# Split fp32r products and gathered experts against plain fp32 products and experts over all tokens

## The reference, cut to what matters

```python
for layer in range(2):                       # first model
    h = rms_norm(x, norm_w)
    proj = h @ w_in                          # 1024 x 12832
    y_a = mamba2_branch(...)                 # convolution, chunked scan, 16 heads
    y_b = sliding_window_branch(...)         # rope, 16 heads, window 128
    y_c = forgetting_attention_branch(...)   # 16 heads
    merged = sum(sigmoid(gate_i) * (y_i @ w_proj[i]))
    x = x + merged @ w_out
x = rms_norm(x, final_norm_w)
# second model: sparse top-64 attention, attention to a memory of 256, S5 state space,
# mixed as above, then the mixture of experts:
combine = ...                                # 256 x 32, two nonzero weights a token
for e in range(32):
    hid = silu(t @ w_gate[e]) * (t @ w_up[e])          # 1024 x 512 each
    out = out + combine[:, e:e + 1] * (hid @ w_down[e])  # 512 x 1024
```

## Time and profile before

| | |
|---|---|
| median of 3 runs | 2602.28 us (2600.16 to 2602.51) |
| profiled execution, own time | 2604.87 us |
| its span | 2603.1 us |
| mean granted clock of PE | 0.888 |
| busy: PE, DVE, ACT, POOL | 2142.0, 1513.6, 1197.3, 898.8 us |
| read from HBM | 406.23 MB |

### The profile page before, as it was taken

One profiled execution on the slowest core, in us unless ns is written; L12 is line 12 of the kernel. 1 busy time (PEld: TensorE's weight loads), 2 busy tenths in 40 slices (PEclk: granted clock), 3 DMA queues, 4 the chain that ended last, 5 costly groups with the idle time before them and its releaser, 6 DMA issues.

```text
span 2603.1 us, 26970 instructions
## 1 busy us (share of the span) xinstructions
PE 2142.0 (82%) x10022; PEld 1737.6 (67%) x10022; DVE 1513.6 (58%) x2250; ACT 1197.3 (46%) x1786; POOL 898.8 (35%) x417
## 2 busy tenths in 40 slices
PE   6796998999878699899765276447689999999997
PEld 5575776677657577667654255335578888888885
DVE  1666232432166623244784645893478888888885
ACT  4342443333333244333324234102457777777774
POOL 4562653346456265334435124643300000000000
PEclk8897998899789799899877687777889999999998
DMA  5342442233434244223333112132469999999994
GB/s 168 99 121 74 131 129 81 81 98 121 130 106 122 74 128 128 77 89 116 105 100 102 49 49 88 66 113 65 145 221 335 328 332 335 322 336 332 324 335 164
DMA packets 137450, 411.15 MB, mean 158 GB/s; under 512 B 20572, under 2 KB 21980, under 8 KB 110184
## 3 DMA queue, kind: packets, MB, share of 16 engines
q1 hardware_dynamic: 132280, 407.31, 47.6%
q0 software_dynamic: 5040, 2.12, 0.3%
HBM read 406.23 MB, written 19.40 MB: 164 GB/s over the span
## 4 chain that ended last, share of the span: by engine, by line
PE 70%; DVE 23%; ACT 4%; issue 2%; DMA 1%; POOL 0%; SPq 0%; DVEq 0%; ACTq 0%; POOLq 0%
PE bank L518 18%; PE bank L519 17%; PE bank L520 17%; DVE r L945 9%; PE bank L830 3%; PE bank L497 2%; DVE small L945 2%; PE bank L598 2%; DVE r L1462 2%; DVE r L951 2%; DVE r L948 1%; DVE scratch L948 1%; PE bank L671 1%; PE bank L689 1%; PE bank L581 1%
## 5 line engine op out<-in xcount | busy, mean ns | idle before, releaser
L2093 POOL TENSOR_TENSOR w_lo<-w_raw,w_hi 128x1024 fp32r<-128x1024 f32 (+2 forms) x348 | 815.6, 2356 | 957.2 <-ACT w_hi L1748 956.8
L1748 ACT CAST w_hi<-w_raw 128x1024 fp32r<-128x1024 f32 (+2 forms) x348 | 350.1, 1014 | 374.9 <-PE bank L520 370.0
L518 PE MATMUL bank<-w_hi,h_hi 128*128 128x512 f32 (+2 forms) x1056 | 441.8, 418 | 83.4 <-POOL w_lo L2093 70.5
L519 PE MATMUL bank<-w_lo,h_hi 128*128 128x512 f32 (+2 forms) x1056 | 425.0, 402 | 0.0
L520 PE MATMUL bank<-w_hi,h_lo 128*128 128x512 f32 (+2 forms) x1056 | 424.7, 402 | 0.0
L518 PEld LDWEIGHTS bank<-w_hi,h_hi 128*128 128x128 f32 x1056 | 217.3, 206 | 140.0 <-POOL w_lo L2093 70.6
L2136 POOL DMA_INDIRECT y_rows<-merged,bias x35 | 38.8, 1107 | 669.1 <-ACT merged L2024 565.1
L1173 DVE TENSOR_REDUCE small<-bank 128x2 f32<-128x512 f32 (+1 forms) x76 | 44.1, 580 | 355.6 <-PE bank L672 165.2
L520 PEld LDWEIGHTS bank<-w_hi,h_lo 128*128 128x128 f32 x1056 | 215.8, 204 | 44.8
L519 PEld LDWEIGHTS bank<-w_lo,h_hi 128*128 128x128 f32 x1056 | 217.3, 206 | 39.2
L1887 ACT ACTIVATE r<-bank,small 128x256 f32<-128x256 f32 (+1 forms) x152 | 63.9, 425 | 337.7 <-DVE small L948 337.7
(11 more groups left out here) (276 smaller groups left out, 4421.4 us busy)
## 6 DMA issues: line engine op xcount, KB each, us to landing
w_raw<-in_w_in SPq DMA_DIRECT2D x236, 512.0 KB, 3.6
r<-in_w_up SPq DMA_DIRECT2D x69, 1024.0 KB, 5.2
w_raw<-in_w_gate SPq DMA_DIRECT2D x68, 1024.0 KB, 5.3
w_raw<-in_w_down SPq DMA_DIRECT2D x36, 1024.0 KB, 5.3
r<-in_w_down SPq DMA_DIRECT2D x34, 1024.0 KB, 5.3
w_raw<-in_w_proj SPq DMA_DIRECT2D x48, 512.0 KB, 3.3
w_raw<-in_w_out SPq DMA_DIRECT2D x24, 512.0 KB, 3.5
w_raw<-in_w_mem_kv SPq DMA_DIRECT2D x8, 512.0 KB, 4.1
```

What stands on the lines that cost most here:

```text
L518: e.matmul(out_, sh, mh, start=first, stop=False, skip_group_check=shared)
L519: e.matmul(out_, sh, ml, start=False, stop=False, skip_group_check=shared)
L1748: a.copy(halves(n)[0], raw_of(n)).then_inc(w_hi, 1)
L2093: g.tensor_tensor(lo, raw_of(n), hi.bitcast(F32), SUB).then_inc(w_lo, 1)
```

## The change

What it does, part by part:
- **Dense products** are one plain fp32 matmul each, from the slot where the weights landed. ACT's casts, POOL's and DVE's low halves and the float32r tiles go. There are 14 raw slots in place of 6, and SP waits for PE instead of POOL.
- **Activations** are transposed and copied once, by DVE where a scale is applied, else by ACT.
- **Experts** run over all 256 tokens. `inner` makes the gate and the up product turned (hidden units on partitions, 256 tokens streamed), DVE multiplies the hidden values by the token's weight for this expert, spread over partitions by 32 small matmuls, and `outer` adds the down product of all 32 experts up in banks 0 to 3. Gathering, blocks, scatter and reload go.
- **Finer steps**: the convolution gives way after each tap, the rope after q and after k; the forgetting gate's logarithm moves from `forget` into `window`. The lists of shares follow.

```diff
-MAMBA = [1, 8, 1, 8, 1, 3, 1, 1, 1] + [1] * 9 + [1]
-WINDOW = [1, 1, 1, 1] + [1] * 18 + [1]
+MAMBA = [2, 2, 2, 2, 1] * 2 + [1, 3, 1, 1, 1] + [1] * 9 + [1]
+WINDOW = [3, 1, 3, 1, 1, 1] + [1] * 18 + [1]
...
-                        n, hi, lo = next_piece()
+                        n, w = next_piece()
                         ends = k0 + PK == c.n_k
                         for t, (b, bank) in enumerate(got):
                             for k in range(PK):
                                 kk = k0 + k
-                                done = product(bank[:, 0:c.n], tuple(a[:, kk, t * P:(t + 1) * P] for a in c.lhs), (hi[:, k, :], lo[:, k, :]),
-                                               kk == 0 and c.bias is None, kk == c.n_k - 1)
+                                done = e.matmul(bank[:, 0:c.n], c.lhs[:, kk, t * P:(t + 1) * P], w[:, k, :], start=kk == 0 and c.bias is None, stop=kk == c.n_k - 1)
...
+                def inner(kind, x):
+
+                    n = matrix_at[kind, x]
+                    e.wait_ge(in_moe[n % PAIRS], 32 * (n // PAIRS + 1))
+                    parts = [by_k(a, 4) for a in slots_of(n)]
+                    for i in range(4):
+                        if i % 2 == 0:
+                            b, bank = take(gates_up[kind], (kind, x, i // 2))
+                        for k in range(KD):
+                            done = e.matmul(bank[:, (i % 2) * S:(i % 2 + 1) * S], parts[k // 4][:, k % 4, i * P:(i + 1) * P], hT[:, k, :], start=k == 0, stop=k == KD - 1)
...
+                def outer(x):
+
+                    n = matrix_at["w_down", x]
+                    e.wait_ge(in_moe[n % PAIRS], 32 * (n // PAIRS + 1))
+                    e.wait_ge(hidden_ready, 2 * (x + 1))
+                    parts = [by_k(a, 2) for a in slots_of(n)]
+                    for t in range(T):
+                        for j in range(2):
+                            for k in range(4):
+                                done = e.matmul(banks[sums[2 * t + j]][:, :], hid[x % 2][:, k, t * P:(t + 1) * P], parts[k // 2][:, k % 2, j * CH:(j + 1) * CH],
+                                                start=x == 0 and k == 0, stop=x == EXP - 1 and k == 3)
...
+                inner("w_gate", 0)
+                inner("w_up", 0)
+                inner("w_gate", 1)
+                weights()
+                inner("w_up", 1)
+                for x in range(EXP):
...
+                    outer(x)
+                    if x + 2 < EXP:
+                        inner("w_gate", x + 2)
+                        inner("w_up", x + 2)
```

More of the change, by code:

```diff
@@ L90, in run, with idle @@
         pass
-def chain(*parts):
-    for p in parts:
-        yield from p
+def idle(n):
+    for _ in range(n):
+        yield
 def bc(ap, n):
@@ L313, in cols_of, with mix_of @@
             return got
-        def mix_of(tag, y3, n_k, wg, wp, bias, first, **ready):
-            yk = tuple(a[:, 0:n_k, :] for a in yT)
-            sp = None if y3 is None else split(tag, y3, yk, n_k, **ready)
+        def mix_of(tag, y3, n_k, wg, wp, bias, first, lhs=None, **ready):
+            yk = lhs if lhs is not None else yT[:, 0:n_k, :]
+            sp = None if y3 is None else Split(tag, y3, yk, n_k, **ready)
             got = []
@@ L370, in build @@
             L.append(e)
-        next(c for c in L[-1]["last"] if c.split is not None and c.split.tag == ("out", LAYERS - 1)).memory = True
         w2 = d["w_in_2"]
@@ L507, in do_split @@
                     e.wait_ge(*s.ready)
-                transposes(("split", s.tag), blocks_of(s.src, s.n_k), min(4, s.n_k))
+                transposes(("split", s.tag), blocks_of(s.src, s.n_k, s.apart), min(4, s.n_k))
             def await_split(s):
-                if s.col0 is None:
-                    await_drained(("split", s.tag, T * s.n_k // min(4, s.n_k) - 1))
-                else:
-                    e.wait_ge(split_made, 4 * s.order)
-            def product(out_, stat_pair, mov_pair, first, last, shared=False):
-                (sh, sl), (mh, ml) = stat_pair, mov_pair
-                e.matmul(out_, sh, mh, start=first, stop=False, skip_group_check=shared)
-                e.matmul(out_, sh, ml, start=False, stop=False, skip_group_check=shared)
-                return e.matmul(out_, sl, mh, start=False, stop=last, skip_group_check=shared)
+                await_drained(("split", s.tag, T * s.n_k // min(4, s.n_k) - 1))
             def next_piece():
@@ L659, in window @@
             def window(l):
-                yield
-                yield
+                yield from idle(4)
                 e.wait_ge(rope_ready, 2 * (l + 1))
@@ L922, in groups_of @@
                 t, k = divmod(g * w, s.n_k)
-                yield g, tuple(a[:, k:k + w, t * P:(t + 1) * P] for a in s.pair), k
-        def idle(n):
-            for _ in range(n):
-                yield
+                yield g, s.dst[:, k:k + w, t * P:(t + 1) * P], k
         @block.vector
@@ new lines, in activate @@
+                def activate(x):
+                    for i in range(2):
+                        b, bank = await_full(("w_gate", x, i))
+                        if x >= 2:
+                            a.wait_ge(hidden_ready, 2 * (x - 1))
+                        a.activation(act[x % 2][:, 2 * i:2 * i + 2, :], by_k(bank[:, :], 2), ACT.Silu).then_inc(drained[b], 1)
+                activate(0)
+                activate(1)
+                for x in range(0, EXP, 2):
+                    copy_out(("weights", x), weight_of(x, 2))
@@ L2046, in scalar_program @@
+                for x in range(2, EXP):
+                    activate(x)
             a.wait_ge(in_consts, 32)
@@ L2130, in ssm @@
                 yield
-            def store_rows(x):
-                for key in (("rows", x // 2), ("down", x, 0), ("down", x, 1)):
-                    b, n = acc[key]
-                    g.wait_ge(drained[b], n)
-                g.indirect_dma_start(d["y_rows"][:, :], bass.IndirectOffsetOnAxis(ap=row_i[:, x:x + 1], axis=0), y_out[x % 2][:, :], None,
-                                     bounds_check=2 * S - 1, oob_is_err=False).then_inc(scattered[x % 2], 16)
-            def moe():
-                for t in range(T):
-                    g.wait_ge(ht_hi_made, t + 1)
-                    g.tensor_tensor(by_k(ht[1][:, t, :], KD), apart(normed3[:, t, :], KD), by_k(ht[0][:, t, :].bitcast(F32), KD), SUB).then_inc(ht_lo_made, 1)
-                for x in range(BLOCKS - 1):
-                    store_rows(x)
-                store_rows(BLOCKS - 1)
-            for l in range(LAYERS):
-                run(dense(L[l]["first"] + L[l]["mamba"] + L[l]["window"] + L[l]["forget"] + L[l]["last"]))
-            run(dense(e2["kmv"] + e2["q"] + e2["sparse"] + e2["memory"]))
-            weave(dense(e2["ssm"]), ssm(), n_pieces(e2["ssm"]), SSM)
-            run(dense(e2["last"]))
-            feed(len(pieces))
-            moe()
+            run(ssm())
         @block.sync
```

590 lines of the change are left out of this document (147 added, 443 removed).

## The result

| | before | after |
|---|---|---|
| median | 2602.24 us (4 runs) | **3174.6 us** (3171.57 to 3179.53, 4 runs) |
| ratio, 95% interval | | **1.2203** (1.2182 to 1.2225) |
| profiled execution, its span | 2604.87, 2603.1 us | 3174.87, 3173.1 us |
| last dense matmul of the layers | 1858.6 us | 1799.1 us |
| from there to the end | 744.5 us | 1374.0 us |

The change makes the kernel 572 us slower: the experts take 629.5 us more (forecast +630), the layers 59.5 us less (forecast -2). The forecast of 3231 is 56 us too high, all of it in the layers.

The account below looks back on a forecast made before the run. The experts were taken as bound by PE, the layers partly by PE and partly by what it waits for. 2604.9 (profiled) + 630 (experts) - 2 (layers) = 3233, given as 3231 since the profiled run stood 2.6 above the median; range 3140 to 3345.

Parts of the forecast that it names:

- The experts: Mixture of experts: 32 experts at 41.4 us, 1324.8, plus head and tail make 1374.3 against 744.5 us, +630.
- The low clock behind the gap: Head of the experts: PE's clock is low after the 10.5 us gap, for which 6 us were added.
- The spreading of the weights: Head of the experts: 32 matmuls 256 wide, 13.8 us, plus 3 of handoffs.
- The layers: All stages before the experts: +235 us of PE work against shorter waits and better clock, stage by stage summing to -2.
- The surcharge: Layers: each of 1312 plain fp32 products costs 0.179 us more than the split one, +235 if all on the path.
- POOL: Layers: PE's 70.5 us of waits for POOL go; 60 DVE operations save 80 us, most of it beside PE.
- Finer steps: Layers: evictions between convolution taps, and six pieces ahead of the rotated q's transposes, where PE idles 18.8 us.
- Stages: Layers, stretch by stretch: changes from waits, clock and longer products, from -22 (memory product) to +13, summing to -2.
- PE-bound throughout: Layers: bound by PE throughout, so the added work lies on the path, +165, time 3396; chance 14%.
- Better cover: Layers: without POOL, DVE's chains shrink, the clock stays up and the layers lose 100, time 3131; chance 12%.
- One record per fp32 matmul: Layers and experts: the second record costs nothing, a product falls from 0.681 to 0.43 us, time 2420; chance 3%.
- DMA or banks hold PE up: Experts: PE is held up by more than 2 us each, time 3231 + 64 or more; chance 3%.

Follow-up runs that it names:

- `pool_tiny`: Kernel before, with POOL's low half of each weight piece cut from 1024 columns to 2 and PE's work kept: 2440.67 us.
- `coarse`: Changed kernel with whole convolutions and ropes, the logarithm back in `forget` and the old shares; products stay plain fp32: 3205.62 us.
- run 35: Not a run number but a cost of 35 us: changed kernel plus one paced 512-column POOL operation per layer weight piece, 3209.7 us.

## Why the prediction was right, and where not

**The experts (+630, measured +629.5): right, term by term in the main.** The period is 41.36 for 41.4, the gap of 10.5 and the transposes of 3.67 came as taken. Three small terms were off and cancelled, which is luck. The router's matmuls took 3.9 us (forecast 6.8), since the clock was 0.91 there and not at half. The low clock behind the gap cost 1.5 (42.9 for gate 0, up 0 and gate 1 instead of 41.4; forecast 6). The spreading of the weights took 25.3, 0.5 of it waiting (forecast 16.8), since the clock fell to 0.50 in it. DVE's routing stayed under the three products. The down product's matmul costs 13.74 / 16 = 0.859 us, against 3 x 0.227 for the split product. With this the four passes of the Trainium skill (FP8 and Floating Point Precision, TensorE Precision Notes) agree: 0.859 / 4 is 0.215. By that section and the Trainium skill's page TensorE: Matmul & The Clock Gate, Back-to-back issue gap, I had estimated a surcharge of 35 us more; no such thing shows, mostly because the split's three passes are 0.227 apart in the trace and not at the page's 0.216.

**The layers (-2, measured -59.5): the mechanisms right, the sizes not, the sum 57 too high.** The experiments lead from one kernel to the other. Each step shows where the layers end, and what it changes in the first layer's Mamba, window and forget stretch and in the memory product:

| step | layers end | change | Mamba | window | forget | memory product |
|---|---|---|---|---|---|---|
| before | 1858.6 | | | | | |
| POOL's work out (`pool_tiny`) | 1693.6 | -165.0 | -24.2 | -5.6 | -17.6 | -10.8 |
| plain fp32 products, no casts, no two-step handoffs (`coarse`) | 1830.9 | +137.3 | +9.2 | +20.5 | +23.4 | -13.8 |
| finer steps (changed kernel) | 1799.1 | -31.8 | +0.2 | -10.8 | -8.9 | 0 |

The middle step adds 235 us of PE work; at 0.68 that is +160, so casts and handoffs give back some 20. That figure is a difference, and no run measured it by itself; but the memory product, which gets 13.8 us shorter with 5.7 us more of PE work, can hold nearly all of it. It is where `pool_tiny` still has a wait of 13.4 us at L518. Of the parts of my sum:
- *The surcharge.* I charged it nearly in full, and let waits and clock give back amounts chosen stage by stage. Over the layers as a whole only 0.68 to 0.72 of added PE work is paid: of 235 us some 70 are covered. In Mamba I charged 26 us, and the whole middle step costs 9.2 there. **This is the term that was sized worst.** What covers the work is not only PE's idle time; the clock that rises with the load is part of it.
- *POOL.* I split it into 70.5 us of PE's waits and some saving on DVE. The split was wrong in both. Without POOL's work 42.6 us of the waits stay, and yet the layers end 165 us earlier. On DVE I counted 60 operations and took their median for their mean: they gave back 58 us (1398 to 426 ns) and not 80, while all of DVE's operations in the layers gave back 244. Where POOL's operations lie beside DVE's chains the total came near (state-space stretch -15, measured -22.2, where `pool_tiny` alone has -24.5; memory product -22, measured -24.5).
- *Finer steps.* I put 18.8 us into each window stretch and none into forget; they gave 10.8 and 9.6 there, and 8.9 and 6.5 in forget.
- *Stages* (forecast, measured): Mamba -6, -14.8 and -12.7; window +3, +4.1; forget +5, -3.1 and -2.6; last stretches +13 and -8, +9.3 and -10.1; q, sparse and memory attention +10, +1.8; last mixture +12, +8.3. The window stretch came right by luck, as POOL gave 5.6 us that I had not put there and the finer steps 8 less than I had. In forget I had the sign wrong: the 17.5 us that I took from idle time and clock came (17.6, with POOL's work out), and the finer steps came on top. In Mamba POOL's work was worth 24.2, less than the 32 that I put there, and the middle step 9.2, far less than the 26.

**The rivals.** PE-bound throughout (3396; its 165 were added to a sum that held -2 already, so it should be 2 us more) fell. Better cover (3131) came half true: the layers end midway between it and the forecast. One record per fp32 matmul (2420) fell by the 0.216 and 0.43 us above. That DMA or banks hold PE up fell: PE stands nowhere before L750.

**What was to show it.** The share of the DMA in the experts is 0.38 for 0.83, POOL is busy for 38.2 us, the 60 DVE operations take 426 ns: as written. The start of the experts, near 1860 by the forecast, came at 1799, 61 us earlier, and I had given 60 as the mark of being wrong: on the layers I was.

## What to carry to other kernels

An fp32 matmul that replaces three float32r ones takes instructions away and gives PE 26% more to do. Count records and distances of starts, not instructions, and then ask what share of PE's time is paid at all (here 0.7). Where POOL works beside DVE, price it by what DVE's operations grow by, not by PE's waits for POOL: work that nobody waited for cost 157 us. Fewer columns help (half of them left 35 of the 157); the same columns in two operations help much less (110 in the changed kernel, and 17 us won in the kernel before). Swap the arithmetic of an algorithm once before giving it up: the all-token experts took 1374 us in fp32, and 512 in bf16, where the loads bound them. Then compare it with its rival at the same arithmetic.

## What was not expected of the hardware

- **The DMA** moved 413 GB/s over 440 us with large loads in flight, where the earlier trace rows had 315. I had used 315 as a limit; the share beside it (0.88) already said that it was not.
- **Noise on POOL** that shares no data with anyone slows DVE's 128x512 operation from 426 to 1021 ns in the mean, and a run of 3175 us by 157. Each of the slow operations starts during one of POOL's and ends 0.28 us after it; the others keep their 0.43. One operation of 512 columns a piece costs the run 35 us, two back to back 110, one of 1024 157; a rule for what the run pays was not found.
- **The clock** can fall under a PE that is never idle: in the row of 64 matmuls over 32 rows (L783) from 1.00 to 0.50, and the distance of starts from 0.216 to 0.427 us. With the 128-row matmuls of L750 behind them it came back. Whether the rows or the spread operand (one column over 128) do it was not tried.
- **The clock rises** with added work: with the fourth matmul the first Mamba stretch went from a clock of 0.89 to 0.96 and grew by 12 us, for 36 pieces x 4 x 0.227 = 33 us of matmuls.
